# Four LayerNorm stops of a two-block transformer kernel, worked by token halves instead of all tokens at once

## The reference

```python
def ffn_sublayer(h, shift, scale, gate, w_in, w_out, g, b):
    y = swiglu(modulate(h, shift, scale), w_in, w_out)
    return layer_norm(ALPHA * h + FFN_RES * gate * y, g, b)

for i in range(DEPTH):                       # DEPTH = 2
    h_lat = ffn_sublayer(h_lat, ...); h_ctx = ffn_sublayer(h_ctx, ...)      # norm 0
    u_lat = modulate(h_lat, m_lat[3], m_lat[4]); u_ctx = modulate(h_ctx, m_ctx[3], m_ctx[4])
    y_lat, y_ctx = attention(u_lat, u_ctx, ...)                             # neighbourhood (i=0), window (i=1)
    h_lat = layer_norm(ALPHA * h_lat + m_lat[5] * y_lat, ...)               # norm 1
    h_lat = ffn_sublayer(h_lat, ...)                                        # norm 2
    if i == 0:
        h_ctx = layer_norm(...); h_ctx = ffn_sublayer(h_ctx, ...)           # norms 1 and 2 for the context
```

## Time and profile before

| what | value |
|---|---|
| median of 3 runs | 2852.09 us (2850.26 to 2857.19) |
| the profiled execution's own time | 2847.28 us |
| its span, first to last instruction | 2845.6 us |
| mean granted TensorE clock | 0.954 |
| PE busy | 2585.0 us, 91% |
| DVE busy | 1648.0 us, 58% |
| ACT busy | 895.3 us, 31% |

### The profile page before, as it was taken

The page is one execution under the profiler, slowest core; times in us unless marked ns, Lnnn a source line. Parts: engine busy times, 40 slices in busy tenths (PEclk is TensorE's granted clock), DMA queues, the critical chain, the costliest instruction groups (busy, mean ns, idle before and its releaser), DMA issues. The chain is left out here.

```text
span 2845.6 us, 37675 instructions
## 1 busy us (share of the span) xinstructions
PE 2585.0 (91%) x14022; PEld 1864.1 (66%) x14022; DVE 1648.0 (58%) x2417; ACT 895.3 (31%) x1421; POOL 222.5 (8%) x372
## 2 busy tenths in 40 slices
PE   5999998998899999899998878997988998798987
PEld 3888885665687887687886557996666433466322
DVE  3877785444587778778777656666543232563101
ACT  1222235443422223422224434445332100443100
POOL 0010002221001110001110001000002000000000
PEclk9999998999899999899998989998989999899998
DMA  7666552332266756457663216554205799516998
GB/s 268 190 190 188 167 182 66 67 75 83 59 192 194 242 173 197 120 179 220 204 190 94 61 47 229 174 168 117 59 8 214 301 427 427 162 47 253 419 428 340
DMA packets 428855, 527.93 MB, mean 186 GB/s; under 512 B 29766, under 2 KB 382532, under 8 KB 416292
## 3 DMA queue, kind: packets, MB, share of 16 engines
q1 hardware_dynamic: 393188, 399.71, 40.8%
q0 software_dynamic: 35520, 126.24, 14.1%
HBM read 524.85 MB, written 1.05 MB: 185 GB/s over the span
## 5 line engine op out<-in xcount | busy, mean ns | idle before, releaser
L1927 DVE TENSOR_TENSOR wlo<-raw,whi 128x1024 fp32r<-128x1024 f32 x392 | 476.5, 1222 | 227.1 <-ACT whi L1456 217.5
L1456 ACT ACTIVATE whi<-raw 128x1024 fp32r<-128x1024 f32 x392 | 413.8, 1058 | 558.1 <-PE bank L714 508.2
L712 PE MATMUL bank<-xhi,whi 128*128 128x512 f32 (+1 forms) x1568 | 571.3, 364 | 3.0 <-DVE xlo L2482 3.0
L713 PE MATMUL bank<-xlo,whi 128*128 128x512 f32 (+1 forms) x1568 | 562.8, 359 | 0.0
L714 PE MATMUL bank<-xhi,wlo 128*128 128x512 f32 (+1 forms) x1568 | 562.4, 359 | 0.0
L1966 DVE SCALAR_TENSOR_TENSOR acc<-mod_ring,conds,acc 128x1024 f32<-128x1024 f32 x308 | 381.5, 1280 | 10.5 <-DMA mod_ring<-in_w_ada 5.4
L712 PEld LDWEIGHTS bank<-xhi,whi 128*128 128x128 f32 x1568 | 296.4, 189 | 63.0 <-issue 20.3
L714 PEld LDWEIGHTS bank<-xhi,wlo 128*128 128x128 f32 x1568 | 296.3, 189 | 44.7
L713 PEld LDWEIGHTS bank<-xlo,whi 128*128 128x128 f32 x1568 | 296.5, 189 | 43.0 <-issue 0.7
L1332 PE MATMUL bank<-experts,gathered 128*64 128x512 f32 (+1 forms) x1024 | 238.7, 621 | 29.6 <-DMA experts<-in_w_up 26.6
L712 PE MATMUL bank<-hhi,whi 128*128 128x512 f32 (+1 forms) x704 | 257.3, 366 | 0.2 <-DVE hlo L2068 0.2
(11 more groups left out here) (316 smaller groups left out, 3319.5 us busy)
## 6 DMA issues: line engine op xcount, KB each, us to landing
raw<-in_ffn_w_in SPq DMA_DIRECT2D x176, 512.0 KB, 4.2
mod_ring<-in_w_mod POOLq DMA_DIRECT2D x128, 512.0 KB, 4.6
experts<-in_w_gate SPq DMA_DIRECT2D x32, 2048.0 KB, 20.9
experts<-in_w_up SPq DMA_DIRECT2D x32, 2048.0 KB, 20.6
experts<-in_w_down SPq DMA_DIRECT2D x32, 2048.0 KB, 20.7
mod_ring<-in_w_ada POOLq DMA_DIRECT2D x96, 512.0 KB, 4.8
raw<-in_ffn_w_out SPq DMA_DIRECT2D x64, 384.0 KB, 3.5
raw<-in_ffn_w_out SPq DMA_DIRECT2D x64, 320.0 KB, 3.1
```

Of the source, the lines that this page charges most:

```text
L712: pe.matmul(o, wh, hi[:, k0 + k, cols], start=(first and k == 0), stop=False)
L713: pe.matmul(o, wh, lo[:, k0 + k, cols], start=False, stop=False)
L1456: act.activation(whi[:, slot, :], raw[:, slot, :], ACT.Copy).then_inc(*n.mark("hi_ready"))
L1927: dve.tensor_tensor(wlo[:, slot, :], raw[:, slot, :], whi[:, slot, :].bitcast(F32), ALU.subtract)\
```

## The change

At the four stops the last two output tiles are no longer made for 512 columns in one go. PE makes both tiles for the latents first, then both for the context from the same weights. The latents' mean is taken within the context's products. DVE centres the latents (bank 4) while PE works on the context, and ACT squares them. Then the second mean (bank 6) follows. DVE's loop over the tiles takes in turns: scale the latents' tile, low part of the latents' tile before the last, centre the context's tile; ACT squares the context's tile in its loop between modulations. PE makes the latents' part of two products tile by tile, then sums the context's squares, then makes the latents' part of the third, and then all of it again for the context. At stop 4 the third product is for the latents alone.

Where a rider runs, `sum_row` moves from ahead of the last unit (u = 15) to ahead of u = 12, and `SLICES[4]` takes the eighth slice at u = 11 instead of 12, with the others closer together. POOL waits for 24 `x_ready` instead of 16, since each tile now counts twice behind stop 1. In the out projection the loop of two times four units becomes six units in a row and the divided tail. The diff, cut to its core:

```diff
-SLICES = {..., 4: (1, 0, 1, 0, 1, 1, 0, 1, 0, 1, 1, 0, 1, 0, 0, 0)}
+SLICES = {..., 4: (1, 0, 1, 1, 0, 1, 0, 1, 1, 0, 1, 1, 0, 0, 0, 0)}
 # PE
+            def stop_by_halves(tiles, lat_banks, ctx_banks, hi, lo, turn=None):
+                slots = []
+                for parts, b in zip(tiles, lat_banks):
+                    acquire(b)
+                    for j, (k0, kt) in enumerate(parts):
+                        slots.append(unit())
+                        product(b, slots[-1], kt, k0, hi, lo, LAT, j == 0, j == len(parts) - 1,
+                                done="half_made" if j == len(parts) - 1 else None)
+                if turn:
+                    turn()
+                for i, (parts, b) in enumerate(zip(tiles, ctx_banks)):
+                    acquire(b)
+                    for j, (k0, kt) in enumerate(parts):
+                        product(b, slots[i * len(parts) + j], kt, k0, hi, lo, CTX, j == 0, j == len(parts) - 1)
+                        if i + j == 0:
+                            mean_of(0)
+                half_squares(0)
+                mean_of(1)
+                half_root(0)
+            def products_by_halves(banks, lat_only=None):
...
+                for g in range(2):
+                    for k in range(KD):
+                        pe.wait_ge(s["x_ready"], before + g * KD + k + 1)
+                        for j, b in enumerate(banks[:2]):
+                            tile(b, slots[j], g, k, k == KD - 1, g * (2 if lat_only and j else 1))
+                    third = lat_only or banks[2]
+                    if g == 0:
+                        half_squares(1)
+                        acquire(third)
+                        slots.append(unit())
+                    if not (g and lat_only):
+                        for k in range(KD):
+                            tile(third, slots[2], g, k, k == KD - 1, g)
+                    if g == 0:
+                        half_root(1)
-                            if on_dve and u == 4 * reps - 1:
+                            if on_dve and u == 4 * reps - (4 if divided else 1):
...
                                 sum_row(rider[3])
 # ACT
+            def halves_modulated(m, scale):
+                for g, c in enumerate(GROUPS):
...
+                    for k in range(KD + 1):
...
+                        if g == 0 and k < KD:
+                            square(1, k)
+                    if g == 0:
+                        half_root(1)
+            def stop_by_halves(early=0, late=AHEAD):
...
+                table_of(ACT.Sqrt)
+                for _ in range(early):
+                    split()
+                for k in range(KD):
+                    square(0, k)
+                for _ in range(late):
+                    split()
+                half_root(0)
 # DVE
+            def stop_by_halves(ks, parts, lat_banks, ctx_banks, m, gate, norm, then, finish, early=0, rider=None):
+                for _ in range(early):
+                    split()
+                for b, k in zip(lat_banks, ks):
+                    dve.wait_ge(*n.next("half_made"))
+                    halved_residual(0, b, m, gate, k)
...
+                for k in range(KD):
+                    center(0, k)
+                for j, (b, k) in enumerate(zip(ctx_banks, ks)):
+                    dve.wait_ge(*n.next("units_done", parts))
+                    halved_residual(1, b, m, gate, k)
+                    if j:
+                        own()
+                        dve.sem_inc(*n.mark("h_ready"))
+                    if not early:
+                        split()
+                half_reciprocal(0)
+                for g, c in enumerate(GROUPS):
...
+                    for k in range(KD + 2):
+                        if k < KD:
+                            dve.scalar_tensor_tensor(h[:, k, c], h[:, k, c], v("ln_g", i + k, 1), bank[b][:, c], ALU.mult, ALU.mult)
...
+                        if k > 1:
+                            low(k - 2, c)
+                        if g == 0 and k < KD:
+                            center(1, k)
+                    if g == 0:
+                        split()
+                        half_reciprocal(1)
 # POOL
-            pool.wait_ge(*n.next("x_ready", 2 * KD))
+            pool.wait_ge(*n.next("x_ready", 3 * KD))
```

More of the change, by code:

```diff
@@ L703, in first_mods, with product @@
                     turn_row(4, first_row)
-            def product(b, slot, kt, k0, hi, lo, cols, first, last, x_wait=False):
+            def product(b, slot, kt, k0, hi, lo, cols, first, last, x_wait=False, done="units_done"):
                 for k in range(kt):
@@ new lines, in half_root @@
+            def half_root(g):
+                rows, b = slice(HD * g, HD * g + HD), NORM_BANKS[g]
+                pe.wait_ge(*n.next("root_ready"))
+                acquire(b)
+                for c in (2 * g, 2 * g + 1):
+                    mm = pe.matmul(bank[b][:, c * P:(c + 1) * P], tab("ident")[rows, 32 * c:32 * c + 1].broadcast_to([HD, P]),
+                                   tmp[rows, 0, 0:P], start=True, stop=True, skip_group_check=True)
+                    if c == 2 * g:
+                        mm.then_inc(s["bank_ready5"], 1)
+                mm.then_inc(s[f"bank_ready{b}"], 1)
@@ L795, in up_down @@
                             continue
+                        divided = cols.stop == T and (kind, half) == ("down", 1)
                         for u in range(4 * reps):
@@ L1530, in up_down @@
                                     loads.extend(next_loads)
+                                if cols.stop == T and (kind, half) == ("down", 1) and step_no == 2 * reps - 2:
+                                    split()
+                                    n.next("units_done", 4)
+                                    mod_row(on_dve)
+                                    for b in range(4):
+                                        n.next(f"bank_read{b}")
+                                    stop_by_halves()
+                                    break
                                 units(1)
@@ L2044, in up_down @@
                             rep, f = step_no // 2, step_no % 2
+                            if divided and step_no == 2 * reps - 2:
+                                split()
+                                stop_by_halves((KD - 2, KD - 1), 2, (0, 1), (2, 3), m, gate, *stop, rider=(rider[0], rider[1], rider[2]))
+                                break
                             if on_dve:
@@ L2099, in layer_norm @@
                 norm_read()
-                if finish:
-                    finish()
                 i = (l * 3 + j) * KD
                 if then:
[L2104 to L2110, removed]
+                    modulated_bias(i, *then)
                 reciprocal_root(cols)
```

217 lines of the change are left out of this document (169 added, 48 removed).

## The result

| | before | changed |
|---|---|---|
| runs, median (range), us | 2851.18 (2850.09 to 2857.19) | 2879.7 (2871.44 to 2882.57) |
| ratio, 95% interval | | 1.0087 (1.0070 to 1.0103) |
| profiled execution, its span, us | 2847.28, 2845.6 | 2871.44, 2869.8 |
| mean granted clock | 0.954 | 0.955 |

The change costs 0.87%, which is 25 us (20 to 29); the forecast was +10. In absolute time it was 2862 in 2844 to 2876. Slower was right, but the median lies 17.7 us above the forecast and 3.7 above the range; by the ratio, 1.0087 times 2851.18, the time is 2876.0, at the range's upper edge.

The account below looks back on a forecast made before the run. PE, busy 91%, was taken as the bound, with 18 us gaps at norm stops. Stops +5.3 - 3.05 + 1.25 + 3.7 = +7.2, plus 2.5 for clock: about +10, 2857 profiled, 2862 with 4.8 for the median; range 2844 to 2876.

Parts of the forecast that it names:

- Shape of a stop: Stop behind a down projection, from unit 11's end: six terms summing to 51.9 us, against 50.7 before at stop 1.
- five places named: Within a stop, saved standing returns: row sum, two half chains, squares on PE's path, DVE-paced pairs, halved matmuls.
- the 4.35: Last context product to first scaling, on DVE's queue: semaphore, residual and sum, split, reciprocal, spread; 4.35 us.
- Row sum: Ahead of the last tiles, PE waits 3.1 us for DVE's eighth slice, then sums for 1.1: 4.2 us.
- the 0.6 us a stop for the clock: Lower clock after a stop's three shorter gaps: 0.6 us a stop, 2.5 in all, bounds 0 and 25.
- rival 3: Lower clock stays through squares and third products: 6.3 us more a stop; 2872 for half, 2885 for all; chance 0.17.
- Rival 1: Row sum doesn't wait for DVE's slice at three stops: 9.3 us less, 2852.5, no change; chance 0.22.
- Stop 1: Behind the first down projection, POOL's start moves 6.35 us later; less 1.0 of slack, +5.3 us.
- Stop 2: Stop without rider or row sum, from unit 5's end: 43.9 us against 47.9, with 0.95 of PE wait -3.05.
- Stop 3: Stop of 51.9 us plus 0.95 of PE waiting for the fourth unit's split, against 51.6: +1.25 us.
- Stop 4: Late splits delay the rotation to 3.85 us behind the products, +3.15; stop in all +3.7, bounds 0.5 and 5.
- Clock inside the pairs: In the product pairs after first scaling, DVE's pace of 1.13 us a tile hides nearly all of a lower clock.

Follow-up runs that it names:

- A: Changed kernel with the row sum moved between the latents' products of the last two tiles: 2860.95 us, ratio 1.0029 to the kernel before.
- F: Changed kernel with 7 idle matmuls ahead of the early row sum, filling its wait: 2872.52 us, ratio 1.0073 to the kernel before.
- B: Changed kernel with POOL's position bias loading released ahead of stop 1: 2874.31 us, ratio 1.0070 to the kernel before.
- H: Changed kernel with idle matmuls in the norm's gaps, ahead of the latents' root and each half's pairs: 2879.06 us, ratio 1.0093 to the kernel before.
- C: Changed kernel with both the row sum between the latents' tiles and the bias loaded ahead of stop 1: 2855.18 us, ratio 1.0009 to the kernel before.
- D: Changed kernel with row sum moved, bias loaded early and stop 4 undivided: 2851.22 us, ratio 0.9987 to the kernel before; once more 2850.43, 0.9997.
- I: Kernel before, undivided, with the row sum three products earlier and the changed kernel's DVE slices: 2865.93 us, ratio 1.0044 to the kernel before.

## Why the prediction was right and wrong

- **Shape of a stop: right.** In terms of the sum, stop 1 measured (end of unit 11 at 410.5): wait 3.31 for 3.1; last tile to first scaling 4.4 for 4.35; last low part of the latents 446.25 - 436.19 = 10.1 for 10.1; squares and spread with the third product 5.7 for 5.35; last low part of the context 461.22 - 453.14 = 8.1 for 8.1. Most of the standing in the middle went (18 us to 7.5), and the time came back in the five places named. Three slips of the sum are small: the parts of the 4.35 add up to 4.25; stop 4 halves 108 pairs, fewer than the 120 to 132 given; and the 3.85 by which stop 4's rotation was to come late does not follow from the terms beside it (three moves of 0.5 would make it 4.1, 0.5 for all three 3.1). Measured are 3.0.
- **Row sum: right place, wrong size.** This is the main step that failed: the step "the row sum itself takes 1.1: 4.2" and the 0.6 us a stop for the clock were too small. I put the clock's cost on gaps in general and on the third products (rival 3), and not on the 3.1 us wait that I had just worked out. A and F give 3.3 of wait and 1.5 to 2.7 behind it at each of three stops: 15.9 us, where the prediction had 9.3 for the waits and 2.5 for the clock in all, over every gap of four stops. Rival 1 had the right mechanism for a repair: with the wait away the kernel stands at +0.29% (A).
- **Stop 1: +11.3 for +5.3.** POOL starts 50.9 us behind unit 11, for 48.25 forecast and 42.0 before: 2.6 of the miss are the lower clock and the terms above. The other 3.3 is a step I did not take at all: I moved POOL's chain by 6.35 us and kept its transfer at 3.53, but it took 6.78, beside weight loads that now came closer together (that these are why is argued, not shown). B removes 6.3 us there.
- **Stop 2: -2.0 for -3.05**, right within the clock's play. **Stop 3: +5.1 for +1.25**, of which 2.7 is the clock behind the row sum (F). **Stop 4: +6.0 for +3.7**, of which 1.5 is. The late rotation made 2.3 of it where the prediction had 3.15. So some 1 us remains at stop 3 and nearly 2 at stop 4 for which no run stands alone.
- **Clock inside the pairs: right** (H), though the granted clock was 0.50 there as feared. Rival 3's case, the lower clock through the third products, did not come at stop 1 (1.00 over 448 to 452, and again from 464 on).
- **The rest, +3.3, is no cost of the change that I can show.** It is what is left of +6.0 in one stretch behind the two blocks and -2.7 elsewhere there. In that stretch the same 742 matmuls took 122.3 us at full clock in the profile of before, and 128.3 at 0.95 in the changed kernel (the same within 0.1 in A, B and C); D and I, with three and no divisions, have it at 1.00. Before, changed, D:

```profile
2479.50:2601.80 122.30, 113.29 (x742) 85.34 (x740) 67.50 (x108) 52.92 (x104) 0.00 (x0) 1.00 0.35 122
```

```profile
2498.30:2626.60 128.30, 119.44 (x741) 88.85 (x740) 67.50 (x108) 53.07 (x105) 0.00 (x0) 0.95 0.34 119
```

```profile
2479.20:2601.70 122.50, 113.24 (x741) 85.28 (x740) 67.49 (x108) 52.91 (x104) 0.00 (x0) 1.00 0.35 123
```

What decides which one a run gets stays open, and so does the +1.9 in the rest of the window attention.

## What to carry over

A wait that an edit creates in a stream that TensorE itself paces can cost twice: its length, and the matmuls behind it at the lower clock until the level rises again; here 3.3 us became 5.0 to 6.1. Where another engine set the pace (H), the lower clock cost at most 0.85 us in stop 1. When an engine's start moves, move its transfers too and look at what is in the queues at the new time, not at the old. And a helper sum that only waits (the row sum) should stand where its input is sure to be ready: one place further down took two thirds of the whole cost away.

## What the runs showed of the hardware

- After 3.3 us of standing the granted clock was 0.74 over 412 to 416 us and the sixteen small matmuls took 1.89 us instead of 1.07; with idle matmuls in the wait it was 1.00 and they took 1.07. At stop 4 the same wait left the row sum itself at 1.07 us, with the fall behind it (0.50 from 1533.5 on): the fall doesn't always come at the same point of a wait.
- In the Trainium skill, the page "TensorE: Matmul & The Clock Gate", section "HAM oscillation — how this bites in real kernels", has bursts parted by waits start at the half rate. The trace agrees at stops 1 and 3, where what followed the wait began at 0.50, and only in part at stop 4, where the row sum still ran at full clock; F against the changed kernel prices it at 1.6, 2.7 and 1.5 us.
- An idle matmul of 256 columns of float32 takes 0.445 us, two passes of 0.222, where a matmul of 256 columns of the split parts takes 0.120.
- The same stretch of code, with the same work and waits, took 122.3 or 128.3 us by the clock that it was granted. So a difference of 6 us between two profiles in a stage that an edit does not touch says nothing on the edit.
